# Tap work of the up stages deferred by one job on VectorE

## The chip, the core and the metric

One NeuronCore of a Trainium2 chip runs the whole program. TensorE (PE) multiplies, VectorE (DVE) and ScalarE (ACT) do the elementwise work, SyncE (SP) issues the loads of weights, GpSimd (POOL) does little here. The metric is the device time of one execution in microseconds, lower is better.

## The reference

Two transformer-like blocks on 256 positions (272 with the 16 meta positions), width 2048, all in float32. The change touches one thing in it, the feed-forward part of the first block, which is done once in each of its two layers:

```python
def causal_dwconv(x, w):
    """Causal depthwise conv over positions. x (B,L,C), w (K,C); tap K-1 = current position."""
    ...
    out = xp[:, 0:L] * w[0]
    for t in range(1, K):
        out = out + xp[:, t:t + L] * w[t]

def conv_ffn(h, w_up, dw, w_down):      # D_FF = 5632, K = 3
    u = causal_dwconv(h @ w_up, dw)
    val, gate = u[..., :D_FF], u[..., D_FF:]
    return (jax.nn.silu(gate) * val) @ w_down
```

## The kernel before

Activations lie transposed, channels on the 128 partitions and positions along the free axis, so that a product makes one tile of 128 output channels by 272 positions (258 in layer 1 of the up stages). Everything is float32, and products are made from rounded halves: a weight tile w becomes w_hi (rounded by ScalarE, line 321) and w_lo = w - w_hi (VectorE, line 327), and each tile of 128 by 128 weights takes three matmuls, x_hi with w_hi, x_lo with w_hi, x_hi with w_lo (lines 359 to 361).

The weights stream through the whole program in **parts** of at most eight 128 by 128 tiles. A part goes through four steps, each on another engine: SP loads it into `raw` (a ring of 4), ScalarE rounds it (`round_part`), VectorE subtracts (`split_part`), TensorE multiplies. `w_hi` and `w_lo` have four slots, and `AHEAD` is 3: when ScalarE and VectorE stand at part v of a stage, they prepare part v + 3, then do what follows from part v. ScalarE may round part v + 3 when TensorE is done with part v - 1. SP loads into a ring slot again when VectorE has split what lay in it.

A layer's feed-forward part is done in two halves of 22 hidden tiles each. So there are four **up stages**, called up00, up01, up10 and up11 (layer, half), each followed by a down stage. An up stage is a hardware loop of 11 iterations. One iteration has four **jobs** of two parts each, that is eight parts and 192 matmuls: u = 0 the gate of hidden tile s = 0, u = 1 its value, u = 2 and 3 the gate and the value of s = 1. Job u ends with part 2u + 1. For every job the two engines have to do this (`ffn_vector` and `ffn_scalar`):

- VectorE scales the product out of PSUM by the root, into `f_raw` (line 681), which also frees the PSUM bank;
- ScalarE makes the tap of the current position from it (line 646);
- VectorE adds the two earlier taps (line 685, two instructions);
- for a value job: ScalarE takes silu of the gate (line 650), VectorE multiplies it with the value into `f_hid` (line 695), ScalarE rounds that to `hid_hi` (line 638), VectorE subtracts to get `hid_lo` (line 672). For s = 0 these last two stand in job 2, for s = 1 they end the iteration.

The order is the order of the program on each engine, written out by `run_phase`: for each part first the preparation of part v + 3, then, if the part ends a job, the work of that job. In ScalarE's program this reads: round, round, work of job u, and so on. No step of one engine can pass an earlier one of the same engine. The down stage's first job multiplies the first 11 hidden tiles of the half, the second the other 11, and TensorE waits there for the last `hid_lo` (`hid_lo_made`). There are two PSUM banks that jobs take in turn, so the product of job u must be scaled out before job u + 2 starts.

Of the kernel before, what the change touches and what calls it, by code (L numbers as in the profile page):

```python
# [16 lines left out]
ALU = mybir.AluOpType  # L17
# [154 lines left out]
def build(nc, a, out):  # L172
# [55 lines left out]
    ps = nc.alloc_psum_tensor("ps", [P, 8, 512], F32)  # L228

    def view(buf, first, *shape):  # L230

        n = 1
        for s in shape:
            n *= s
        v = buf[:, first:first + n]
        if len(shape) == 1:
            return v
        names = "abcd"[:len(shape)]
        return v.rearrange(f"p ({' '.join(names)}) -> p {' '.join(names)}", **dict(zip(names, shape)))

    def col(name, tile=0):

        first = VOFF[name]
        if isinstance(tile, int):
            return vec[:, first + tile:first + tile + 1]
        return vec[:, first:][:, bass.ds(tile, 1)]
# [10 lines left out]
    drained = [sem(f"drained{b}") for b in range(2)]  # L257
# [69 lines left out]
        nc.vector.tensor_tensor(w_lo[:, j % SLOTS, 0:kt], raw[:, j % RING, 0:kt],  # L327
                                w_hi[:, j % SLOTS, 0:kt].bitcast(F32), ALU.subtract).then_inc(split, 1)

    def run_phase(eng, p, work, prepare, last=False):  # L330

        def body(i, on):
            for v, (u, k0, _) in enumerate(p.parts):
                if on or v + AHEAD < len(p.parts):
                    prepare(eng, p, i, v + AHEAD, p.ahead[v])
                if v == p.last[u] and work is not None:
                    work(i, u)
        n = p.n - 1 if last else p.n
        if n == 1:
            body(0, True)  # L340
        elif n > 1:
            with eng.Fori(0, n) as i:
                body(i, True)
        if last:
            body(p.n - 1, False)

    def result_ready(eng, p, i, u):

        eng.wait_ge(multiplied, i * len(p.parts) + (p.base + p.last[u] + 1 + SLOTS))
# [20 lines left out]
    def bank(name, u):  # L370
        return (results[name][0] + u) % 2
# [91 lines left out]
    def tile_of(buf, first, i, per):  # L463

        if isinstance(i, int):
            return buf[:, first + per * i]
        return buf[:, first:][:, bass.ds(i * per, 1)].rearrange("p a t -> p (a t)")
# [136 lines left out]
    f_raw, f_root = view(arena, FT0 + 8 * T, 2, T), arena[:, FT0 + 10 * T:FT0 + 11 * T]  # L604
# [22 lines left out]
    def ffn_tap(layer, f, t, is_gate, i, s):  # L627

        return col("ffn_dw", i * 2 + ((layer * FFN_K + t) * 2 * FF + is_gate * FF + f * FH + s))

    def ffn_scalar(act, layer, f):
# [8 lines left out]
        def work(i, u):  # L640
# [10 lines left out]
            if u == 3:  # L651
                high(i, 1)
        run_phase(act, p, work, round_part)
        name2 = f"down{layer}{f}"

        def squares(i, u):
            if u % 2:
# [3 lines left out]
                else:  # L661
                    square_tile(act, name2, i, u // 2, 2, 0)
        run_phase(act, ph[name2], squares if f else None, round_part)

    def ffn_vector(dve, layer, f):
        name, n0 = f"up{layer}{f}", (2 * layer + f) * FH
        p = ph[name]
        w, c = T - TAIL * layer, (FFN_K - 1) * layer

        def low(i, s):  # L670
            dve.wait_ge(hid_hi_made, i * 2 + (n0 + s + 1))
            nc.vector.tensor_tensor(tile_of(hid_lo[layer], s, i, 2)[:, 0:w - c], f_hid[:, s, c:w],  # L672
                                    tile_of(hid_hi[layer], s, i, 2)[:, 0:w - c].bitcast(F32), ALU.subtract).then_inc(hid_lo_made, 1)

        def work(i, u):
            s, is_gate = u // 2, 1 - u % 2
            if u == 2:
                low(i, 0)
            dst, raw_ = (f_gate if is_gate else f_val), f_raw[:, u % 2]
            result_ready(dve, p, i, u)  # L680
            nc.vector.tensor_tensor(raw_[:, 0:w], ps[:, bank(name, u), 0:w], f_root[:, 0:w], ALU.mult).then_inc(drained[bank(name, u)], 1)  # L681
            dve.drain()  # L682
            dve.wait_ge(hid_tap, i * 4 + (2 * n0 + u + 1))
            for back in (1, 2):
                mm = nc.vector.scalar_tensor_tensor(out=dst[:, s, back:w], in0=raw_[:, 0:w - back],  # L685
                                                    scalar=ffn_tap(layer, f, 2 - back, is_gate, i, s),
                                                    in1=dst[:, s, back:w], op0=ALU.mult, op1=ALU.add)
                if back == 1:
                    dve.drain()
            if is_gate:  # L690
                mm.then_inc(hid_tapped, 1)
            else:
                dve.drain()
                dve.wait_ge(hid_silu, i * 2 + (n0 + s + 1))
                nc.vector.tensor_tensor(f_hid[:, s, c:w], f_act[:, s, c:w], f_val[:, s, c:w], ALU.mult).then_inc(hid_made, 1)
            if u == 3:
                dve.drain()
                low(i, 1)
        run_phase(dve, p, work, split_part)
        name2 = f"down{layer}{f}"  # L700
        p2 = ph[name2]

        def low_input(i, s):


            dve.wait_ge(x0_hi_made, i * 2 + (s + 1))
            nc.vector.scalar_tensor_tensor(out=tile_of(x0_lo, s, i, 2), in0=tile_of(h, s, i, 2)[:, META:T],
                                           scalar=col("norm_w_2", i * 2 + s), in1=tile_of(x0_hi, s, i, 2).bitcast(F32),
                                           op0=ALU.mult, op1=ALU.subtract).then_inc(x0_lo_made, 1)

        def add(i, u):
            if u == 2 and layer and f:
                low_input(i, 0)
            if u % 2:
                result_ready(dve, p2, i, u)
                t = tile_of(h, u // 2, i, 2)[:, META * layer:T]
                nc.vector.tensor_tensor(t, ps[:, bank(name2, u // 2), 0:T - META * layer], t, ALU.add).then_inc(drained[bank(name2, u // 2)], 1)
            if u == 3 and layer and f:
                dve.drain()
                low_input(i, 1)  # L720
        run_phase(dve, p2, add, split_part)
# [2036 lines left out]
    with block:  # L2758
# [25 lines left out]
        @block.vector  # L2784
        def _(dve):
            start_vector(dve)
            late_vector(dve)
            dve.wait_ge(seg_made, 1)
            ab_vector(dve)
            dve.wait_ge(norm_std, 2)  # L2790
            for f in range(2):
                ffn_vector(dve, 0, f)
            meet(dve, "ffn0")
            norm_vector(dve, 2, 0, lambda k: col("norm_mix", DK + k), hi=xm_hi, lo=xm_lo)
            mid_vector(dve)
            dve.wait_ge(norm_std, 4)
            for f in range(2):
                ffn_vector(dve, 1, f)
            two_vector(dve)
            meet(dve, "out")  # L2800
            norm_vector(dve, 6, META, lambda k: col("final_norm_w_2", k), lambda k: xn[:, k, 0:S2])
            end_keep(dve, 0)
# [47 lines left out]
```

## Time and profile before

| | us |
|---|---|
| median of three runs | 3663.02 |
| lowest, highest run | 3645.42, 3664.07 |
| the profiled execution | 3644.57 |
| its span in the trace | 3642.9 |
| TensorE busy | 3506.8 (96%) |
| VectorE busy | 2364.7 (65%) |
| ScalarE busy | 1850.9 (51%) |

The profiled execution lies at the low end of the runs. The four up stages start at 409.6, 804.8, 1978.7 and 2360.8 us of the span and last 261, 260, 258 and 255 us, together 1035 us. Busy shares say what an engine does over the whole span. They don't say which engine's order sets the pace of a loop in which the engines wait for each other; for that one follows one iteration in the timeline.

### The profile page before, as it was taken

To read this page: it belongs to the slowest core of one execution; us is meant where nothing else is said; L and a number is where in the kernel's file an instruction comes from. 1 tells how busy PE (TensorE), PEld (TensorE's weight loads), DVE (VectorE), ACT (ScalarE), POOL (GpSimd) and SP (SyncE) were. 2 spreads that over 40 slices of the span, in tenths; PEclk is the share of its full clock that TensorE was granted. 3 is DMA by queue.
4 is the path that set the end of the run, shared out by engine and by line. 5 is a ranking of instruction groups with operands and counts; after the bars stand their busy time and mean duration, and the time that the engine had idled before them with its cause. 6 is when DMAs were issued, how large, how long until landed. Compare 5 with 4: busy or idle time off the path is not lost.

```text
span 3642.9 us, 76660 instructions
## 1 busy us (share of the span) xinstructions
PE 3506.8 (96%) x29352; PEld 3424.9 (94%) x29352; DVE 2364.7 (65%) x3504; ACT 1850.9 (51%) x2670; POOL 307.4 (8%) x363
## 2 busy tenths in 40 slices
PE   8989999999999899999989999999998999999998
PEld 7989999999999898888889999999997999999998
DVE  5987666657765544666656666567667657756555
ACT  4655655444444534444435555444565455475443
POOL 2761200000000000000004000000022000000000
PEclk9999999999999999999999999999998999999999
DMA  5545566566656544222225665766565556557774
GB/s 159 167 144 163 165 177 173 167 188 174 174 172 176 158 136 112 59 59 59 59 59 164 177 178 170 204 179 184 164 189 140 162 162 163 162 151 191 194 195 139
DMA packets 1103744, 561.77 MB, mean 154 GB/s; under 512 B 23044, under 2 KB 1101462, under 8 KB 1103526
## 3 DMA queue, kind: packets, MB, share of 16 engines
q1 hardware_dynamic: 1102309, 554.58, 54.1%
q8 instruction: 143, 2.34, 0.3%
q0 software_dynamic: 624, 2.13, 0.2%
q10 hardware_dynamic: 608, 2.23, 0.2%
q14 instruction: 60, 0.48, 0.0%
HBM read 556.77 MB, written 2.10 MB: 153 GB/s over the span
## 4 chain that ended last, share of the span: by engine, by line
issue 63%; PE 23%; DVE 6%; POOLq 3%; DVEq 2%; ACT 2%; DMA 0%; POOL 0%; ACTq 0%; SPq 0%
PE ps L359 5%; PE ps L360 5%; PE ps L361 5%; PE ps L443 2%; PE ps L444 2%; DVE w_lo L327 2%; PE ps L445 2%; POOLq L489 2%; DVE arena L860 1%; DVEq L682 1%; POOLq L938 1%; DVEq L854 1%; ACT w_hi L321 1%; DVE arena L685 1%; ACT arena L646 0%
## 5 line engine op out<-in xcount | busy, mean ns | idle before, releaser
L327 DVE TENSOR_TENSOR w_lo<-raw,w_hi 128x1024 fp32r<-128x1024 f32 (+1 forms) x1136 | 1351.3, 1206 | 712.2 <-ACT w_hi L321 703.2
L321 ACT ACTIVATE w_hi<-raw 128x1024 fp32r<-128x1024 f32 (+1 forms) x1136 | 1132.5, 1014 | 471.0 <-PE ps L445 249.9
L359 PE MATMUL ps<-x_hi,w_hi 128*128 128x272 f32 (+1 forms) x2816 | 804.1, 286 | 1.3 <-DVE w_lo L327 1.3
L360 PE MATMUL ps<-x_lo,w_hi 128*128 128x272 f32 (+1 forms) x2816 | 802.9, 285 | 0.0
L361 PE MATMUL ps<-x_hi,w_lo 128*128 128x272 f32 (+1 forms) x2816 | 802.8, 285 | 0.0
L443 PE MATMUL ps<-x_hi,w_hi 128*128 128x256 f32 (+2 forms) x2512 | 715.7, 285 | 45.6 <-DVE w_lo L327 31.0
L444 PE MATMUL ps<-x_lo,w_hi 128*128 128x256 f32 (+2 forms) x2512 | 706.9, 281 | 0.0
L445 PE MATMUL ps<-x_hi,w_lo 128*128 128x256 f32 (+2 forms) x2512 | 706.6, 281 | 0.0
L359 PEld LDWEIGHTS ps<-x_hi,w_hi 128*128 128x128 f32 x2816 | 533.7, 190 | 3.4 <-DVE w_lo L327 3.2
L361 PEld LDWEIGHTS ps<-x_hi,w_lo 128*128 128x128 f32 x2816 | 533.7, 190 | 0.0
L360 PEld LDWEIGHTS ps<-x_lo,w_hi 128*128 128x128 f32 x2816 | 533.7, 190 | 0.0
L443 PEld LDWEIGHTS ps<-x_hi,w_hi 128*128 128x128 f32 (+1 forms) x2512 | 475.8, 189 | 53.7 <-DVE w_lo L327 26.6
L444 PEld LDWEIGHTS ps<-x_lo,w_hi 128*128 128x128 f32 (+1 forms) x2512 | 476.4, 190 | 0.4
L445 PEld LDWEIGHTS ps<-x_hi,w_lo 128*128 128x128 f32 (+1 forms) x2512 | 476.3, 190 | 0.3
L359 PE MATMUL ps<-hid_hi,w_hi 128*128 128x272 f32 (+1 forms) x1408 | 398.7, 283 | 4.7 <-DVE hid_lo L672 4.7
L360 PE MATMUL ps<-hid_lo,w_hi 128*128 128x272 f32 (+1 forms) x1408 | 397.9, 283 | 0.0
L361 PE MATMUL ps<-hid_hi,w_lo 128*128 128x272 f32 (+1 forms) x1408 | 397.8, 283 | 0.0
L443 PE MATMUL ps<-xm_hi,w_hi 128*128 128x272 f32 (+2 forms) x944 | 290.6, 308 | 14.5 <-DVE xm_lo L584 8.6
L685 DVE SCALAR_TENSOR_TENSOR arena<-arena,vec 128x271 f32<-128x271 f32 (+1 forms) x352 | 173.9, 494 | 171.7 <-ACT arena L646 141.8
L646 ACT ACTIVATE arena<-arena,vec 128x272 f32<-128x272 f32 (+1 forms) x176 | 91.1, 517 | 379.5 <-DVE arena L681 379.5
L445 PE MATMUL ps<-xm_hi,w_lo 128*128 128x272 f32 (+2 forms) x944 | 275.7, 292 | 0.0
L444 PE MATMUL ps<-xm_lo,w_hi 128*128 128x272 f32 (+2 forms) x944 | 275.1, 291 | 0.0
(553 smaller groups left out, 5409.3 us busy)
## 6 DMA issues: line engine op xcount, KB each, us to landing
raw<-ffn_w_up SPq DMA_DIRECT2D x352, 512.0 KB, 4.5
raw<-w_in SPq DMA_DIRECT2D x232, 512.0 KB, 3.8
raw<-cd_w_in SPq DMA_DIRECT2D x100, 512.0 KB, 3.8
raw<-ffn_w_down SPq DMA_DIRECT2D x128, 384.0 KB, 3.5
raw<-ab_w_in SPq DMA_DIRECT2D x80, 512.0 KB, 3.9
raw<-ffn_w_down SPq DMA_DIRECT2D x128, 320.0 KB, 3.3
raw<-w_out SPq DMA_DIRECT2D x48, 512.0 KB, 4.3
raw<-ab_w_out SPq DMA_DIRECT2D x32, 512.0 KB, 4.0
```

The source lines that it names most:

```text
L321: nc.scalar.activation(w_hi[:, j % SLOTS, 0:kt], raw[:, j % RING, 0:kt], ACT.Copy).then_inc(rounded, 1)
L327: nc.vector.tensor_tensor(w_lo[:, j % SLOTS, 0:kt], raw[:, j % RING, 0:kt], w_hi[:, j % SLOTS, 0:kt].bitcast(F32), ALU.subtract).then_inc( ...
L359: nc.tensor.matmul(acc, w_hi[:, j % SLOTS, k, 0:w], mh, start=first, stop=False)
L360: nc.tensor.matmul(acc, w_hi[:, j % SLOTS, k, 0:w], ml, start=False, stop=False)
L361: last = nc.tensor.matmul(acc, w_lo[:, j % SLOTS, k, 0:w], mh, start=False, stop=end)
L443: nc.tensor.matmul(acc, w_hi[:, j % SLOTS, k, 0:w], mh, start=(k0 + k == 0), stop=False)
L444: nc.tensor.matmul(acc, w_hi[:, j % SLOTS, k, 0:w], ml, start=False, stop=False)
L445: last = nc.tensor.matmul(acc, w_lo[:, j % SLOTS, k, 0:w], mh, start=False, stop=(k0 + k == kt - 1))
L489: pool.drain()
L646: nc.scalar.activation((f_gate if is_gate else f_val)[:, s, 0:w], f_raw[:, u % 2, 0:w], ACT.Copy, scale=ffn_tap(layer, f, 2, is_gate, i, s ...
L682: dve.drain()
L685: mm = nc.vector.scalar_tensor_tensor(out=dst[:, s, back:w], in0=raw_[:, 0:w - back], scalar=ffn_tap(layer, f, 2 - back, is_gate, i, s), i ...
```

## The change

In the up stages VectorE's work of a job is divided. Scaling out of PSUM stays where it was, at the end of the job's second part (`work`). The wait for ScalarE's tap, the two taps, the product with silu, and for s = 0 the subtraction to `hid_lo`, go into a new function `taps` and a new hook `early`, which `run_phase` calls behind the preparation at the first part of a job: the taps of job u - 1 are then done inside job u, between the low weights of its first part's turn and those of its second part's turn. Job 3 is finished at once as before. ScalarE's, TensorE's and SP's programs are the same.

```diff
--- before.py
+++ after.py
@@ -327,12 +327,14 @@
         nc.vector.tensor_tensor(w_lo[:, j % SLOTS, 0:kt], raw[:, j % RING, 0:kt],
                                 w_hi[:, j % SLOTS, 0:kt].bitcast(F32), ALU.subtract).then_inc(split, 1)
 
-    def run_phase(eng, p, work, prepare, last=False):
+    def run_phase(eng, p, work, prepare, last=False, early=None):
 
         def body(i, on):
             for v, (u, k0, _) in enumerate(p.parts):
                 if on or v + AHEAD < len(p.parts):
                     prepare(eng, p, i, v + AHEAD, p.ahead[v])
+                if v == p.first[u] and early is not None:
+                    early(i, u)
                 if v == p.last[u] and work is not None:
                     work(i, u)
         n = p.n - 1 if last else p.n
@@ -672,14 +674,9 @@
             nc.vector.tensor_tensor(tile_of(hid_lo[layer], s, i, 2)[:, 0:w - c], f_hid[:, s, c:w],
                                     tile_of(hid_hi[layer], s, i, 2)[:, 0:w - c].bitcast(F32), ALU.subtract).then_inc(hid_lo_made, 1)
 
-        def work(i, u):
+        def taps(i, u):
             s, is_gate = u // 2, 1 - u % 2
-            if u == 2:
-                low(i, 0)
             dst, raw_ = (f_gate if is_gate else f_val), f_raw[:, u % 2]
-            result_ready(dve, p, i, u)
-            nc.vector.tensor_tensor(raw_[:, 0:w], ps[:, bank(name, u), 0:w], f_root[:, 0:w], ALU.mult).then_inc(drained[bank(name, u)], 1)
-            dve.drain()
             dve.wait_ge(hid_tap, i * 4 + (2 * n0 + u + 1))
             for back in (1, 2):
                 mm = nc.vector.scalar_tensor_tensor(out=dst[:, s, back:w], in0=raw_[:, 0:w - back],
@@ -693,10 +690,22 @@
                 dve.drain()
                 dve.wait_ge(hid_silu, i * 2 + (n0 + s + 1))
                 nc.vector.tensor_tensor(f_hid[:, s, c:w], f_act[:, s, c:w], f_val[:, s, c:w], ALU.mult).then_inc(hid_made, 1)
+
+        def early(i, u):
+            if u:
+                taps(i, u - 1)
+            if u == 3:
+                low(i, 0)
+
+        def work(i, u):
+            result_ready(dve, p, i, u)
+            nc.vector.tensor_tensor(f_raw[:, u % 2, 0:w], ps[:, bank(name, u), 0:w], f_root[:, 0:w], ALU.mult).then_inc(drained[bank(name, u)], 1)
             if u == 3:
                 dve.drain()
+                taps(i, 3)
+                dve.drain()
                 low(i, 1)
-        run_phase(dve, p, work, split_part)
+        run_phase(dve, p, work, split_part, early=early)
         name2 = f"down{layer}{f}"
         p2 = ph[name2]
```

What stands in a row on VectorE shows it. The rows name the line, the operation and its tiles; 128x1024 is the splitting of a whole part, and the register rows (ISA, REGISTER_ALU) set up addresses and the values to wait for. First, in the loop of up00, the stretch from the end of job 0's second part to the end of job 1, in the kernel before:

```order
L327 TENSOR_TENSOR w_lo<-raw,w_hi 128x1024
L349 REGISTER_ALU
L681 TENSOR_TENSOR arena<-ps,arena 128x272
L683 ISA
L685 ISA
L685 SCALAR_TENSOR_TENSOR arena<-arena,vec 128x271
L685 ISA
L685 SCALAR_TENSOR_TENSOR arena<-arena,vec 128x270
L327 TENSOR_TENSOR w_lo<-raw,w_hi 128x1024
L326 REGISTER_ALU
```

and in the changed kernel, where line 702 is the scaling and line 682 the taps:

```order
L327 TENSOR_TENSOR w_lo<-raw,w_hi 128x1024
L351 REGISTER_ALU
L702 TENSOR_TENSOR arena<-ps,arena 128x272
L327 TENSOR_TENSOR w_lo<-raw,w_hi 128x1024
L680 ISA
L682 ISA
L682 SCALAR_TENSOR_TENSOR arena<-arena,vec 128x271
L682 ISA
L682 SCALAR_TENSOR_TENSOR arena<-arena,vec 128x270
L326 REGISTER_ALU
L327 TENSOR_TENSOR w_lo<-raw,w_hi 128x1024
```

The two taps of job 0 stood directly behind its scaling, ahead of both splits of job 1; now one split stands ahead of them and one behind.

Second, the stretch from job 2's second split to the taps of job 2 and on to job 3, before:

```order
L327 TENSOR_TENSOR w_lo<-raw,w_hi 128x1024
L672 ISA
L672 TENSOR_TENSOR hid_lo_85<-arena,hid_hi_83 128x272
L349 REGISTER_ALU
L681 TENSOR_TENSOR arena<-ps,arena 128x272
L683 REGISTER_ALU
L685 ISA
L685 SCALAR_TENSOR_TENSOR arena<-arena,vec 128x271
L685 ISA
L685 SCALAR_TENSOR_TENSOR arena<-arena,vec 128x270
L327 TENSOR_TENSOR w_lo<-raw,w_hi 128x1024
L326 REGISTER_ALU
```

and now (line 674 is the subtraction to `hid_lo`):

```order
L327 TENSOR_TENSOR w_lo<-raw,w_hi 128x1024
L351 REGISTER_ALU
L702 TENSOR_TENSOR arena<-ps,arena 128x272
L327 TENSOR_TENSOR w_lo<-raw,w_hi 128x1024
L680 REGISTER_ALU
L682 ISA
L682 SCALAR_TENSOR_TENSOR arena<-arena,vec 128x271
L682 ISA
L682 SCALAR_TENSOR_TENSOR arena<-arena,vec 128x270
L674 ISA
L674 TENSOR_TENSOR hid_lo_85<-arena,hid_hi_83 128x272
L326 REGISTER_ALU
L327 TENSOR_TENSOR w_lo<-raw,w_hi 128x1024
```

The subtraction for s = 0 has moved from ahead of job 2's scaling to behind the taps of job 2, and these stand between the two splits of job 3. From job 3's scaling to the loop's end the order is the same.

## Rows read from the trace of the kernel before

**Rows 1.** The page: busy time of each engine.

```profile
PE 3506.8 (96%) x29352; PEld 3424.9 (94%) x29352; DVE 2364.7 (65%) x3504; ACT 1850.9 (51%) x2670; POOL 307.4 (8%) x363
```

**Rows 2.** Windows: up01, then up11; length, busy PE PEld DVE ACT POOL, clock, DMA.

```profile
804.80:1065.20 260.40, 260.40 (x2114) 260.40 (x2113) 181.84 (x261) 124.73 (x173) 0.00 (x0) 1.00 0.61 175
...
2360.80:2616.00 255.20, 255.20 (x2114) 255.20 (x2113) 179.44 (x261) 123.35 (x173) 0.00 (x0) 1.00 0.62 179
```

**Rows 3.** The page: costliest groups, up-stage matmuls and weight loads; last field idle before.

```profile
L359 PE MATMUL ps<-x_hi,w_hi 128*128 128x272 f32 (+1 forms) x2816 | 804.1, 286 | 1.3 <-DVE w_lo L327 1.3
...
L359 PEld LDWEIGHTS ps<-x_hi,w_hi 128*128 128x128 f32 x2816 | 533.7, 190 | 3.4 <-DVE w_lo L327 3.2
```

**Rows 4.** Timeline of PEld in up10; start, duration, idle before and its releaser.

```profile
2080.48 0.19 PEld L359 LDWEIGHTS ps<-x_hi,w_hi 128*128 128x128 f32 x1 [0.17 <-DVE w_lo L327]
...
2104.13 0.19 PEld L359 LDWEIGHTS ps<-x_hi,w_hi 128*128 128x128 f32 x1 [0.38 <-DVE w_lo L327]
```

**Rows 5.** Timeline of VectorE in up00, one iteration of the loop.

```profile
561.37 0.43 DVE L681 TENSOR_TENSOR arena<-ps,arena 128x272 f32<-128x272 f32 x1
562.63 0.50 DVE L685 SCALAR_TENSOR_TENSOR arena<-arena,vec 128x271 f32<-128x271 f32 x1 [0.82 <-ACT arena L646]
...
563.72 2.36 DVE L327 TENSOR_TENSOR w_lo<-raw,w_hi 128x1024 fp32r<-128x1024 f32 x2
565.99 0.43 DVE L681 TENSOR_TENSOR arena<-ps,arena 128x272 f32<-128x272 f32 x1
...
569.82 2.36 DVE L327 TENSOR_TENSOR w_lo<-raw,w_hi 128x1024 fp32r<-128x1024 f32 x2 [0.51 <-ACT w_hi L321]
572.09 0.43 DVE L672 TENSOR_TENSOR hid_lo<-arena,hid_hi 128x272 f32 x1
572.45 0.44 DVE L681 TENSOR_TENSOR arena<-ps,arena 128x272 f32<-128x272 f32 x1
...
577.04 0.44 DVE L681 TENSOR_TENSOR arena<-ps,arena 128x272 f32<-128x272 f32 x1
578.28 0.50 DVE L685 SCALAR_TENSOR_TENSOR arena<-arena,vec 128x271 f32<-128x271 f32 x1 [0.80 <-ACT arena L646]
...
579.60 0.44 DVE L695 TENSOR_TENSOR arena<-arena 128x272 f32<-128x272 f32 x1
...
585.27 0.43 DVE L681 TENSOR_TENSOR arena<-ps,arena 128x272 f32<-128x272 f32 x1
```

**Rows 6.** Timeline of ScalarE in up00, the same iteration.

```profile
561.94 0.52 ACT L646 ACTIVATE arena<-arena,vec 128x272 f32<-128x272 f32 x1 [1.93 <-DVE arena L681]
562.37 2.00 ACT L321 ACTIVATE w_hi<-raw 128x1024 fp32r<-128x1024 f32 x2
...
567.11 1.28 ACT L650 ACT_TABLE_LOAD   x1
568.40 0.43 ACT L650 ACTIVATE arena<-arena 128x272 f32<-128x272 f32 x1
568.74 1.99 ACT L321 ACTIVATE w_hi<-raw 128x1024 fp32r<-128x1024 f32 x2
```

**Rows 7.** Timeline of VectorE in up01.

```profile
947.05 0.44 DVE L681 TENSOR_TENSOR arena<-ps,arena 128x272 f32<-128x272 f32 x1 [0.64 <-PE ps L361]
...
953.96 0.43 DVE L681 TENSOR_TENSOR arena<-ps,arena 128x272 f32<-128x272 f32 x1
```

**Rows 8.** Timeline of PE at the end of up00.

```profile
676.94 0.40 PE L359 MATMUL ps<-hid_hi,w_hi 128*128 128x272 f32 x1 [1.79 <-DVE hid_lo L672]
```

**Rows 9.** Timeline of PE at the end of up01.

```profile
1069.74 0.39 PE L359 MATMUL ps<-hid_hi,w_hi 128*128 128x272 f32 x1 [0.26 <-DVE hid_lo L672]
```

**Rows 10.** Timeline of VectorE at the end of up00.

```profile
672.66 0.44 DVE L681 TENSOR_TENSOR arena<-ps,arena 128x272 f32<-128x272 f32 x1
```

**Rows 11.** Windows: just after that gap of PE, columns as in Rows 2.

```profile
677.60:681.10 3.50, 3.50 (x18) 3.50 (x18) 1.76 (x3) 0.91 (x3) 0.00 (x0) 0.51 0.35 105
```

## The prediction

> **What bounds the kernel now.** The page first: TensorE is busy for 96% of the span [rows 1]. Then the up stages by windows: in up01 and up11 it is busy for every microsecond [rows 2]. One iteration is 260.4 / 11 = 23.68 us there and 255.2 / 11 = 23.20 us in up11, whose tiles are 258 wide. A job is a quarter of that, 5.92 us, a part 2.96. Over all four up stages the matmuls waited 1.3 us and the weight loads 3.2 us for w_lo, 4.5 us together [rows 3]. So in these 1035 us there is next to nothing to win, and the question is the other one: how near are VectorE and ScalarE to being late?
>
> For that the timeline of one iteration in up00 is read, both engines side by side [rows 5, 6]. VectorE's scalings of jobs 0, 1, 2, 3, 0 start at 561.37, 565.99, 572.45, 577.04 and 585.27: steps of 4.62, 6.46, 4.59 and 8.23, together 23.90 us. None of these rows has an idle time that PE ended. The two engines turn in a ring, each waiting for the other, and the ring takes 23.90 us where TensorE takes 23.68. It falls back 0.22 us an iteration, living on the lead it had at the stage's start. In up10 the ring is 23.65, which is the distance of two waits of PEld for w_lo [rows 4], against PE's 23.20. The first of them is in the fifth iteration, 101.8 us into the stage: the lead was about 3 x 0.45, 1.4 us, from the second iteration on. In up01 and up11 the ring is shorter, since ScalarE loads no table there, and the scaling waits for PE (0.64 us, [rows 7]).
>
> **The change part by part.** It adds and removes no work that counts; it changes what stands in the ring. The steps, all from the rows:
> - scaling to ScalarE's tap: 561.37 to 561.94, 0.57. Tap to the next round: 562.37, 0.43 [rows 5, 6].
> - round to its split: 568.74 to 569.82, 1.08; ScalarE's second round is ready when VectorE wants it. Split to the next instruction: two take 569.82 to 572.09, so 1.14 each.
> - two taps to the next instruction: 562.63 to 563.72, 1.09. Taps to the product with silu: 578.28 to 579.60, 1.32. Subtraction to hid_lo to the next: 572.09 to 572.45, 0.36, and the product, of the same length and kind, is taken at the same.
> - silu with its table load: 565.99 to 568.40, 2.41 behind the scaling, and the round 0.34 later.
>
> Before, the taps of job 0 lie beside ScalarE's rounding: scaling, 1.26 to the taps, 1.09, then two splits, 2.28: 4.62. Now VectorE has the first split ahead of the taps, and that split needs the round, which ScalarE starts only after its tap. The taps no longer lie beside the round but behind it:
> - job 0 to 1: 0.57 + 0.43 + 1.08 + 1.14 (split) + 1.09 (taps) + 1.14 (split) = **5.45**, was 4.62.
> - job 1 to 2: 2.41 + 0.34 + 1.08 + 1.14 + 1.32 + 0.36 + 1.14 = **7.79**, was 6.46. Job 2's hid_hi is no obstacle: ScalarE makes it while VectorE does the second split.
> - job 2 to 3: 5.45 and the subtraction, 0.36 = **5.81**, was 4.59.
> - job 3 to 0: job 3 is finished at once, so **8.23** as before.
>
> The ring is 27.28 us in up00, 3.60 longer than PE's 23.68; in up10 it is taken as 0.25 less by its narrower tiles, as now (23.65 for 23.90), so 27.03, against 23.20: 3.83. In up01 and up11 ScalarE loads no table: silu can follow the tap by 0.43, as the round does in [rows 6], at 1.00 instead of 2.41, and job 3 to 0 is 947.05 to 953.96, 6.91 [rows 7]. So 5.45 + 6.38 + 5.81 + 6.91 = 24.55, which is 0.87 over 23.68; in up11 24.30, 1.10 over 23.20. There the changed ring comes out as the longer one too.
>
> What PE then waits for w_lo, at the same place in each iteration (the fourth part, whose split is the first behind the 8.23 or 6.91):
> - up00 and up10: the lead of 1.4 goes in the first iteration, which also loses about 2.4 (the first three steps, 0.83 + 1.33 + 1.22, less what was slack while PE still set the pace). 1 us and 9 x 3.60 = 33.4; 1 and 9 x 3.83 = 35.5.
> - up01 and up11: the lead is larger. The first split of job 0 starts 2.28 ahead of 953.96, at 951.68, and ends 1.22 later (2.36 - 1.14), at 952.90; PE ended the iteration just ahead of 947.05, by an estimated 0.2 us of hand-over at 946.85, and wants the fourth part 8.88 later, at 955.73. Lead 2.8 us. Ten iterations at 0.87 and 1.10, the first one less (0.4) and the second more (0.4, from a scaling that no longer catches up), make 8.7 and 11.0, less 2.8: 5.9 and 8.2.
>
> Together 83.0, less the 4.5 there was: **+78.5 us**.
>
> At a stage's end TensorE waits for the last hid_lo: 1.79 us in up00 and 0.26 in up01 [rows 8, 9], a little more in layer 1. In up00 the last scaling starts at 672.66 [rows 10], 1.7 us after the product is there, because the ring is behind. In the changed ring it is 2.28 + 5.45 + 7.79 + 5.81 = 21.33 after the fourth part's split begins; PE starts that part 1.28 after the same moment and has the job's result five parts later, at 1.28 + 14.8 + 0.2 = 16.28. Late by 5.05, 3.4 more than now. In up01: 2.28 + 5.45 + 6.38 + 5.81 = 19.92, late by 3.6 where it was not late. The down stage's first job covers 11 tiles, as now, and all of the addition shows: 2 x 3.4 + 2 x 3.7 = **+14.2 us**. After that gap of PE in up00 the clock was granted at half, 1.2 GHz, for a stretch: 18 matmuls in 3.5 us [rows 11] where 28 go in at a part's pace (24 in 2.96), some 1.3 us lost. With longer gaps I count two more such stretches, **+2.6**, bounds 0 and 5.2.
>
> VectorE's 0.82 us of idle time ahead of the taps [rows 5] goes for three jobs of four, and is worth nothing: it was beside ScalarE's rounding. PSUM banks: scaling is never over 5.1 us late, and a job lasts 5.92, so the bank wait is near but doesn't bind. Loads: a slot of raw is reloaded when its part is split, four parts ahead, over 8 us before ScalarE wants it.
>
> Sum: 78.5 + 14.2 + 2.6 = **+95 us**. Against the profiled execution's 3644.57 that is 3740; the median of the runs is 18 us above that execution, and nothing in the trace says which of the two levels the next runs take. I put the sum on the median, two of three runs being there: **3758 us**.
>
> **Rivals.**
> - *Only the stages with table loads are slowed.* The margin of 0.87 in up01 is a sum of ten steps, and if waits overlap by 0.1 each the lead lasts. Then 5.9 + 8.2 go: 3744.
> - *The clock.* A gap of 3.6 us in each iteration of up00 and up10 may halve PE's clock each time, as at the end of up00 [rows 11]. In my sum the loss is free, since after each gap PE has nothing but the ring to wait for and 3.6 us to catch up in. If it delays the scaling that the ring needs, each costs 1.3 us: 20 x 1.3 = 26, giving 3784. For it: the bank that job 3 leaves is free only 5.92 - 5.05 = 0.9 us before PE wants it. Against: a PE that runs later wants it later too, and the nearest result that the ring needs, job 1's, is there 3.3 us ahead (1.28 + 2.96 + 0.2 against 2.28 + 5.45).
> - *Not slower.* If ScalarE's round were done before VectorE asks for it, the split would cost the ring nothing, the wait of 0.82 us would be filled and the ring shorter than PE's time in every stage. Then the 4.5 us and what up00 and up10 are late by at their ends (2 x 1.7) go: 3655. It decides at the round: it would have to start ahead of the tap, and ScalarE's program puts it behind [rows 6]. A lead could also hide it, but it would have to be 36 us in up00; it is 1.4.
>
> The Trainium skill (TensorE: Matmul & The Clock Gate, "HAM oscillation — how this bites in real kernels") describes a loop whose wait in every turn puts the clock back to half each time. By it the second rival is right about the clock; by the sum it would cost nothing, by the rival 26 us. One gap in the trace agrees; none in a loop is there to look at.
>
> **How the numbers follow.** Forecast 0.70, only two stages 0.09, clock 0.10, not slower 0.11. The range: each iteration's excess is a sum of steps read to 0.02 us, and 0.3 us of error in 40 iterations is 12 us either way; the lower level of the runs takes 18 off. Low: 3758 - 18 - 14 - 12 = 3714. High: 3784 + 12 = 3796. The third rival stays out. A difference under 0.5%, some 18 us, can't be told from no change; only the third rival falls within it (faster by 0.2%), or beyond it where the next runs take the lower level, 3637. So slower 0.89, and of the rival's 0.11 same 0.08, faster 0.03.
>
> **What would show it.** Right: in up00 of the changed profile, steps of scalings near 5.45, 7.8, 5.8 and 8.2; PE idle 3.6 us once an iteration ended by w_lo, in all four stages; ScalarE's idle ahead of its tap longer by about 0.8; last hid_lo waits of 5 us. Wrong: VectorE's taps starting before the first split could be had, steps that sum to under 23.7 us, or a loop time in up01 that stays at 23.68. An error in what PE does in its gaps would show as granted clock under 1 with the iteration longer than 27.3 us.

## The result and the profile after

The changed kernel takes 3752.79 us in the median of four runs (3735.94 to 3759.50), the kernel before 3655.15 us (3645.42 to 3664.07, four runs with one more than were shown). The ratio is 1.027, interval 1.0243 to 1.0297: slower by 97.6 us in the medians, where 95 had been summed. Three single executions of kernels further below (4950, 6930 and 8878 us, where the others of the same kernel lie within 30 us) are in no ratio. The profiled execution of the changed kernel has a span of 3748.9 us, 106 more than the one before.

The page of the changed kernel first, its engine shares and the two rows that answer to [rows 3] (lines 361 and 327 are what lines 359 and 327 were; the last field is the idle time before and its releaser):

```profile
PE 3549.8 (95%) x29352; PEld 3462.5 (92%) x29352; DVE 2354.9 (63%) x3504; ACT 1850.6 (49%) x2670; POOL 306.3 (8%) x363
...
L361 PE MATMUL ps<-x_hi,w_hi 128*128 128x272 f32 (+1 forms) x2816 | 817.1, 290 | 53.9 <-DVE w_lo L327 53.8
...
L361 PEld LDWEIGHTS ps<-x_hi,w_hi 128*128 128x128 f32 x2816 | 543.6, 193 | 61.8 <-DVE w_lo L327 60.9
```

The matmuls of the up stages now wait 53.8 us for w_lo and the weight loads 60.9 us, where it was 1.3 and 3.2. The weight load and the matmul behind it wait at the same time (at 580.28 us both end their wait, after 3.43 and 3.21 us), so the two fields must not be added; the prediction did that with the 4.5 us of before, which was up to 1.3 us too much.

VectorE in one iteration of up00, the answer to [rows 5]. Start, duration, then in brackets the idle time before and what ended it; line 702 is the scaling, 682 the taps, 692 the product, 674 the subtraction to `hid_lo`:

```profile
567.26 0.43 DVE L702 TENSOR_TENSOR arena<-ps,arena 128x272 f32<-128x272 f32 x1
569.34 1.23 DVE L327 TENSOR_TENSOR w_lo<-raw,w_hi 128x1024 fp32r<-128x1024 f32 x1 [1.64 <-ACT w_hi L321]
570.48 0.49 DVE L682 SCALAR_TENSOR_TENSOR arena<-arena,vec 128x271 f32<-128x271 f32 x1
571.14 0.50 DVE L682 SCALAR_TENSOR_TENSOR arena<-arena,vec 128x270 f32<-128x270 f32 x1 [0.17 <-issue]
571.56 0.44 DVE L674 TENSOR_TENSOR hid_lo<-arena,hid_hi 128x272 f32 x1
571.91 1.22 DVE L327 TENSOR_TENSOR w_lo<-raw,w_hi 128x1024 fp32r<-128x1024 f32 x1
573.05 0.44 DVE L702 TENSOR_TENSOR arena<-ps,arena 128x272 f32<-128x272 f32 x1
...
581.28 0.44 DVE L702 TENSOR_TENSOR arena<-ps,arena 128x272 f32<-128x272 f32 x1
...
586.73 0.43 DVE L702 TENSOR_TENSOR arena<-ps,arena 128x272 f32<-128x272 f32 x1
590.55 1.22 DVE L327 TENSOR_TENSOR w_lo<-raw,w_hi 128x1024 fp32r<-128x1024 f32 x1 [3.39 <-ACT w_hi L321]
...
594.50 0.43 DVE L702 TENSOR_TENSOR arena<-ps,arena 128x272 f32<-128x272 f32 x1
```

The scalings of jobs 2, 3, 0, 1 and 2 start at 567.26, 573.05, 581.28, 586.73 and 594.50: steps of 5.79, 8.23, 5.45 and 7.77 us. Before the first split of jobs 3, 1 and 2 VectorE is idle for 1.64 or 3.39 us for ScalarE's rounding, and the taps follow that split without any wait. ScalarE's side (line 648 is the tap):

```profile
587.30 0.52 ACT L648 ACTIVATE arena<-arena,vec 128x272 f32<-128x272 f32 x1 [3.02 <-DVE arena L702]
587.84 1.28 ACT L652 ACT_TABLE_LOAD   x1
589.14 0.43 ACT L652 ACTIVATE arena<-arena 128x272 f32<-128x272 f32 x1
589.47 1.99 ACT L321 ACTIVATE w_hi<-raw 128x1024 fp32r<-128x1024 f32 x2
```

587.30 is the tap of job 1, 0.57 behind the scaling; then the table load, silu, and only at 589.47 the round that VectorE's split waits for at 590.55. The wait of VectorE for the tap, 0.82 us in [rows 5], is gone from jobs 0 to 2. In its place stands a longer wait for the round, and it lies in the ring.

TensorE in up00 at the fourth part of five iterations running, with what it had waited for:

```profile
525.80 0.60 PE L361 MATMUL ps<-x_hi,w_hi 128*128 128x272 f32 x1 [3.22 <-DVE w_lo L327]
...
553.04 0.39 PE L361 MATMUL ps<-x_hi,w_hi 128*128 128x272 f32 x1 [1.91 <-DVE w_lo L327]
...
580.28 0.59 PE L361 MATMUL ps<-x_hi,w_hi 128*128 128x272 f32 x1 [3.21 <-DVE w_lo L327]
...
607.52 0.39 PE L361 MATMUL ps<-x_hi,w_hi 128*128 128x272 f32 x1 [1.85 <-DVE w_lo L327]
...
634.76 0.60 PE L361 MATMUL ps<-x_hi,w_hi 128*128 128x272 f32 x1 [3.22 <-DVE w_lo L327]
```

Waits of about 3.2 and 1.9 us take turns. What stands behind that is shown by windows of the same places (length, busy and count of PE, PEld, DVE, ACT, POOL, granted clock, DMA):

```profile
580.00:583.40 3.40, 3.12 (x14) 3.12 (x15) 1.76 (x4) 1.54 (x3) 0.00 (x0) 0.50 0.45 129
607.40:610.80 3.40, 3.28 (x26) 3.28 (x27) 1.75 (x4) 1.71 (x3) 0.00 (x0) 1.00 0.52 147
```

Behind the 3.2 us wait at 580.28 PE runs at half clock, 0.50, 1.2 GHz: 14 matmuls in 3.4 us. Behind the 1.85 us wait at 607.52 it doesn't. The slow stretch makes PE later, so the next wait is shorter: 3.21 then 1.85. The pace stays the ring's: from 525.80 to 580.28 and from there to 634.76 it is 54.48 us each, two iterations of 27.24.

In up10 it doesn't take turns. Behind the fourth parts at 2081.87, 2108.81, 2135.75, 2162.70 and 2189.65 the clock fell every time, after waits of 3.26, 1.98 and three times 2.13 us; behind the next one, 2.12 us at 2216.59, it did not:

```profile
2108.81 0.39 PE L361 MATMUL ps<-x_hi,w_hi 128*128 128x258 f32 x1 [1.98 <-DVE w_lo L327]
...
2216.59 0.39 PE L361 MATMUL ps<-x_hi,w_hi 128*128 128x258 f32 x1 [2.12 <-DVE w_lo L327]
```

```profile
2109.20:2112.60 3.40, 3.40 (x18) 3.40 (x18) 1.77 (x3) 2.23 (x3) 0.00 (x0) 0.50 0.62 177
2216.60:2220.00 3.40, 3.40 (x28) 3.40 (x29) 1.77 (x3) 1.85 (x3) 0.00 (x0) 1.00 0.54 156
```

So the length of the wait alone doesn't say here whether the clock falls. And with a slow stretch in each of five iterations running they still take 26.94 us each, the time of the ring.

At the ends of up00 and up01, the answer to [rows 8, 9] (in up10 and up11 the same wait is 4.26 and 4.04 us, and was 2.16 and 0.48):

```profile
713.53 0.59 PE L361 MATMUL ps<-hid_hi,w_hi 128*128 128x272 f32 x1 [3.59 <-DVE hid_lo L674]
...
1114.74 0.39 PE L361 MATMUL ps<-hid_hi,w_hi 128*128 128x272 f32 x1 [3.72 <-DVE hid_lo L674]
```

### The profile page after: what moved, and what is told of

Same layout as the page of the kernel before. It is cut to its first block, busy times and chain, and to the rows that moved or that the text cites. A ratio compares the mean times of both kernels' runs of the same rounds, so it can differ in the third digit from the quotient of the medians.

```text
span 3748.9 us, 76528 instructions
## 1 busy us (share of the span) xinstructions
PE 3549.8 (95%) x29352; PEld 3462.5 (92%) x29352; DVE 2354.9 (63%) x3504; ACT 1850.6 (49%) x2670; POOL 306.3 (8%) x363
## 3 DMA queue, kind: packets, MB, share of 16 engines
q0 software_dynamic: 624, 2.13, 0.2%
## 4 chain that ended last, share of the span: by engine, by line
issue 65%; PE 14%; DVE 9%; DVEq 5%; ACT 4%; POOLq 3%; ACTq 0%; DMA 0%; POOL 0%
DVE w_lo L327 4%; ACT w_hi L321 3%; DVEq L686 2%; PE ps L361 2%; PE ps L363 2%; PE ps L362 2%; PE ps L445 2%; PE ps L446 2%; PE ps L447 2%; POOLq L491 2%; DVE arena L869 1%; POOLq L947 1%; DVE arena L682 1%; DVE arena L702 1%; DVEq L863 1%
## 5 line engine op out<-in xcount | busy, mean ns | idle before, releaser
L361 PE MATMUL ps<-x_hi,w_hi 128*128 128x272 f32 (+1 forms) x2816 | 817.1, 290 | 53.9 <-DVE w_lo L327 53.8
L362 PE MATMUL ps<-x_lo,w_hi 128*128 128x272 f32 (+1 forms) x2816 | 811.5, 288 | 0.0
L363 PE MATMUL ps<-x_hi,w_lo 128*128 128x272 f32 (+1 forms) x2816 | 811.4, 288 | 0.0
L361 PEld LDWEIGHTS ps<-x_hi,w_hi 128*128 128x128 f32 x2816 | 543.6, 193 | 61.8 <-DVE w_lo L327 60.9
L362 PEld LDWEIGHTS ps<-x_lo,w_hi 128*128 128x128 f32 x2816 | 543.3, 193 | 0.1
L363 PEld LDWEIGHTS ps<-x_hi,w_lo 128*128 128x128 f32 x2816 | 542.7, 193 | 0.0
L361 PEld LDWEIGHTS ps<-hid_hi,w_hi 128*128 128x128 f32 x1408 | 267.5, 190 | 16.6 <-issue 16.4
```

What stands on the lines that cost most here:

```text
L361: nc.tensor.matmul(acc, w_hi[:, j % SLOTS, k, 0:w], mh, start=first, stop=False)
L362: nc.tensor.matmul(acc, w_hi[:, j % SLOTS, k, 0:w], ml, start=False, stop=False)
L363: last = nc.tensor.matmul(acc, w_lo[:, j % SLOTS, k, 0:w], mh, start=False, stop=end)
```

## The experiments

Eight kernels. All timings are against the kernel before on the same chip, 19 runs of it for the first four kernels and 29 for the others. To set the up stages apart from the rest, I also took from each trace the time from the start of a stage's first matmul to the start of the last matmul of the down stage behind it, and VectorE's scaling starts, whose four steps make the ring:

| kernel | ratio (interval) | up and down stages, us: 00, 01, 10, 11 | sum less before | steps in up00, us | ring in up00, up01, up10, up11 |
|---|---|---|---|---|---|
| before | 1 | 395.0, 391.1, 382.0, 377.6 | 0 | 4.62, 6.45, 4.59, 8.23 | 23.90, 23.68, 23.66, 23.20 |
| changed | 1.027 (1.0243 to 1.0297) | 430.6, 401.3, 417.7, 390.6 | +94.5 | 5.45, 7.78, 5.79, 8.23 | 27.24, 24.50, 26.94, 24.21 |
| taps_ahead | 0.9989 (0.9970 to 1.0008) | 399.7, 391.1, 387.7, 378.2 | +11.0 | 4.62, 6.10, 5.35, 8.24 | 24.32, 23.68, 23.66, 23.20 |
| taps_behind | 1.0255 (1.0221 to 1.0288) | 431.8, 403.1, 421.6, 389.6 | +100.4 | 5.45, 7.78, 5.79, 8.23 | 27.24, 24.60, 26.94, 24.20 |
| scalar_deferred | 0.9954 (0.9934 to 0.9974) | 391.2, 391.1, 380.2, 378.3 | -4.9 | 3.71, 5.82, 5.92, 8.24 | 23.68, 23.68, 23.20, 23.04 |
| gates_only | 1.0104 (1.0074 to 1.0133) | 412.3, 391.1, 399.8, 376.9 | +34.4 | 5.45, 6.10, 5.79, 8.23 | 25.56, 23.68, 25.31, 23.20 |
| after_no_tables | 1.0111 (1.0079 to 1.0143) | 403.6, 402.4, 393.6, 391.9 | +45.8 | 5.45, 6.35, 5.79, 6.90 | 24.49, 24.50, 24.21, 24.21 |
| before_no_tables | 0.9988 (0.9968 to 1.0007) | 392.8, 391.1, 381.5, 378.3 | -2.0 | 4.93, 5.92, 5.92, 6.91 | 23.68, 23.68, 23.20, 23.04 |
| second_halves | 1.0080 (1.0056 to 1.0103) | 395.1, 402.6, 383.2, 392.7 | +27.9 | 4.62, 6.10, 4.95, 8.23 | 23.90, 24.60, 23.66, 24.21 |
| scalar_deferred_no_tables | 0.9983 (0.9963 to 1.0004) | 391.2, 391.1, 377.0, 376.9 | -9.5 | 4.92, 5.92, 5.92, 6.92 | 23.68, 23.68, 23.20, 23.20 |

Where the ring reads 23.68, 23.20 or 23.04 TensorE sets the pace, and so it does in up00 of taps_ahead with 24.32. Two things move a stage by 1 to 7 us between profiled executions, also where no edit touches it: a stretch at half clock at its start, and the pace of its matmuls at full clock (last section). A difference of that size in one stage says little by itself.

### The place of the taps: taps_ahead and taps_behind

The theory says that the loss comes from one thing: the first split, which waits for ScalarE's round, stands between ScalarE's tap and VectorE's taps. taps_ahead moves the hook by one line, ahead of the preparation:

```diff
             for v, (u, k0, _) in enumerate(p.parts):
+                if v == p.first[u] and early is not None:
+                    early(i, u)
                 if on or v + AHEAD < len(p.parts):
                     prepare(eng, p, i, v + AHEAD, p.ahead[v])
-                if v == p.first[u] and early is not None:
-                    early(i, u)
```

> The changed kernel with one thing put back: in the next job VectorE does the deferred taps ahead of the first split instead of behind it. Ring theory: the taps again lie beside ScalarE's rounding, the steps between scalings are again about 4.6, 6.1, 5.0 and 8.2 us, 23.9 in all, and the time is that of the kernel before within 5 us, ratio 1.000. Rival, that it is the division of a job's work into two places that costs (ScalarE's silu and hid_hi later), wherever the taps stand: the loss stays, ratio 1.027.

Measured 0.9989. VectorE in taps_ahead, from a scaling of job 0 to that of job 1:

```profile
589.96 0.43 DVE L702 TENSOR_TENSOR arena<-ps,arena 128x272 f32<-128x272 f32 x1
591.22 0.50 DVE L682 SCALAR_TENSOR_TENSOR arena<-arena,vec 128x271 f32<-128x271 f32 x1 [0.83 <-ACT arena L648]
591.90 0.50 DVE L682 SCALAR_TENSOR_TENSOR arena<-arena,vec 128x270 f32<-128x270 f32 x1 [0.17 <-issue]
592.31 2.35 DVE L327 TENSOR_TENSOR w_lo<-raw,w_hi 128x1024 fp32r<-128x1024 f32 x2
594.58 0.43 DVE L702 TENSOR_TENSOR arena<-ps,arena 128x272 f32<-128x272 f32 x1
```

The steps are back at 4.62 and 6.10 in the same deferred form, and the wait for the tap is back too, so that the work is divided costs nothing by itself. The stages took 11.0 us more than before, though, where 5 had been allowed. In up00 TensorE took 24.32 us an iteration, some 7 us over the stage, with no wait for w_lo in it. Up10 began with a stretch at half clock (13 matmuls from 1987.00 to 1990.00 us of the span, where the kernel before has 27 in 3 us), and its down stage had 342 matmuls in 40 us at full clock where the kernel before has 355. Neither is a wait of the ring; see the last section.

taps_behind puts the taps further on, behind both splits:

```diff
-                if v == p.first[u] and early is not None:
+                if v == p.last[u] and early is not None:
                     early(i, u)
```

> The changed kernel with the deferred taps moved further, behind both splits of the next job and just ahead of its scaling. Ring theory: a sum of the same steps (tap 0.57, round 0.43, 1.08, split, split, taps), so again about 5.45, 7.8, 5.8, 8.2 us and 27.25 in all, and the time of the changed kernel, ratio 1.027. Rival, that what costs is the second part's low weights coming later because the taps stand between the two splits: they are early again, ratio 1.00 to 1.005.

Measured 1.0255, and the steps of up00 are those of the changed kernel to 0.01 us. VectorE in taps_behind:

```profile
580.11 0.43 DVE L702 TENSOR_TENSOR arena<-ps,arena 128x272 f32<-128x272 f32 x1
582.19 2.36 DVE L327 TENSOR_TENSOR w_lo<-raw,w_hi 128x1024 fp32r<-128x1024 f32 x2 [1.65 <-ACT w_hi L321]
584.47 0.49 DVE L682 SCALAR_TENSOR_TENSOR arena<-arena,vec 128x271 f32<-128x271 f32 x1
585.14 0.50 DVE L682 SCALAR_TENSOR_TENSOR arena<-arena,vec 128x270 f32<-128x270 f32 x1 [0.17 <-issue]
585.56 0.44 DVE L702 TENSOR_TENSOR arena<-ps,arena 128x272 f32<-128x272 f32 x1
```

Both splits are now made in a row, the second part's low weights a good microsecond earlier than in the changed kernel, and it doesn't help. It is the sum of what stands in the ring that counts, not its order, as long as the first split is ahead of the taps.

### Taking the round out of the ring: scalar_deferred

If the loss is that ScalarE's round stands behind its tap, then deferring ScalarE's tap as well, to between its two rounds, must take it away and more:

```diff
-        def work(i, u):
-            s, is_gate = u // 2, 1 - u % 2
-            if u == 2:
-                high(i, 0)
+        def tap(i, u):
+            s, is_gate = u // 2, 1 - u % 2
             result_out(act, name, i, u)
...
-            if u == 3:
-                high(i, 1)
-        run_phase(act, p, work, round_part)
+        def early(i, u):
+            if u:
+                tap(i, u - 1)
+
+        def work(i, u):
+            if u == 2:
+                high(i, 0)
+            if u == 3:
+                tap(i, 3)
+                high(i, 1)
+        run_phase(act, p, work, round_part, early=early)
```

> The changed kernel, and ScalarE's tap and silu of a job deferred likewise: between its two rounds of the next job. Then the first round does not stand behind the tap. Ring theory: scaling 0.43, split 1.14, taps 1.09, split 1.14, so 3.8 for a gate job, about 5.0 for job 1 to 2, 4.2 for 2 to 3, 8.2 at the loop's end: 21.2 us, under TensorE's 23.68 and 23.20 in all four stages. The waits for low weights go, and the ends of up00 and up10 look like those of up01 and up11: 8 us under the kernel before, ratio 0.998. Rival, that VectorE's deferral costs by itself (PSUM banks or hid_lo late): ratio stays near 1.027.

VectorE in up00 of scalar_deferred (line 709 is the scaling, 689 the taps), and the page's row of the up stages' matmuls:

```profile
559.86 0.43 DVE L709 TENSOR_TENSOR arena<-ps,arena 128x272 f32<-128x272 f32 x1
560.22 1.21 DVE L327 TENSOR_TENSOR w_lo<-raw,w_hi 128x1024 fp32r<-128x1024 f32 x1
561.35 0.49 DVE L689 SCALAR_TENSOR_TENSOR arena<-arena,vec 128x271 f32<-128x271 f32 x1
562.02 0.50 DVE L689 SCALAR_TENSOR_TENSOR arena<-arena,vec 128x270 f32<-128x270 f32 x1 [0.17 <-issue]
562.43 1.22 DVE L327 TENSOR_TENSOR w_lo<-raw,w_hi 128x1024 fp32r<-128x1024 f32 x1
563.57 0.43 DVE L709 TENSOR_TENSOR arena<-ps,arena 128x272 f32<-128x272 f32 x1
...
569.38 0.44 DVE L709 TENSOR_TENSOR arena<-ps,arena 128x272 f32<-128x272 f32 x1 [0.50 <-PE ps L363]
```

```profile
L361 PE MATMUL ps<-x_hi,w_hi 128*128 128x272 f32 (+1 forms) x2816 | 802.6, 285 | 0.0
```

The step from job 0 to job 1 is 559.86 to 563.57, 3.71 where 3.8 was summed, and the next scaling waits for PE, 0.50 us. The matmuls have no idle time before them. At the end of up00 PE waits 0.27 us for hid_lo where it was 1.79 [rows 8]. The measured ratio, 0.9954, is even better than the 0.998 expected; the stages themselves gave 4.9 us, 0.13%, so most of the 17 us in the ratio does not come from there, and I don't claim it for the edit. Of the 8 us forecast, 5.6 came in up00 and up10 (3.8 and 1.8), and there up10's down stage had 342 matmuls in 40 us at full clock where the kernel before has 355. It beats the changed kernel by some 3% and is not slower than the kernel before.

### Half the dose: gates_only

```diff
         def early(i, u):
-            if u:
+            if u % 2:
                 taps(i, u - 1)
...
-            if u == 3:
+            if u % 2:
                 dve.drain()
-                taps(i, 3)
+                taps(i, u)
```

> Only the gate jobs (0 and 2) are deferred, the value jobs are finished at once. Ring theory: steps of 5.45, 6.1, 5.8, 8.2 us, 25.6 in all in up00 and 25.35 in up10, 1.9 and 2.15 over TensorE's time, so 18 and 20 us of waits for low weights and 1.7 at each end; in up01 and up11 the ring is 23.4 and 23.1, just under TensorE's time, so nothing. In all 38 us over the kernel before, ratio 1.010. Rival, a cost in proportion to the jobs deferred: two of three, 65 us, ratio 1.018.

Measured 1.0104, interval to 1.0133: the ring's 38 us, not the 65 of a cost by count. The stages lose 34.4 us: 17.3 and 17.8 in up00 and up10, and in up01 and up11 nothing, as the sum of 23.4 and 23.1 had it, under TensorE's time by 0.3 and 0.1. So a step that makes the ring longer is free up to TensorE's time and is paid in full from there on.

### The table loads: after_no_tables and before_no_tables

One line ahead of the loops of up00 and up10 brings in silu's table, so that the loop's body has no load (`warm` is a column of its own):

```diff
+        if not f:
+            nc.scalar.activation(warm[:, 0:1], eps[:, 0:1], ACT.Silu)
```

> The changed kernel with one silu of a single column on ScalarE ahead of up00 and of up10, so that the loops start with silu's table and load none in their iterations. Ring theory: the ring of up00 and up10 becomes that of up01 and up11, 24.5 and 24.2 us instead of 27.25 and 26.95, so these two stages lose what up01 and up11 lose: 48 us less than the changed kernel, ratio to before 1.0135. Rival, that the table loads are idle time of an engine that has enough of it (ScalarE is busy for half of the span) and another wait takes their place: under 10 us of change, ratio 1.025.

> The kernel before with the same single silu ahead of up00 and up10. Ring theory: the ring falls from 23.9 to 21.3 us, TensorE sets the pace in all four stages, the 4.5 us of waits for low weights and 3.4 us at the ends of up00 and up10 go: 8 us less, ratio 0.998. Rival, that the table loads cost nothing here: ratio 1.000, and the waits for w_lo still there in the profile.

In the changed kernel up00 with its down stage then takes 403.6 us and up01 402.4; the rings are 24.49 and 24.50. 45.8 us over the kernel before is left of 94.5, ratio 1.0111, in whose interval the expected 1.0135 lies. ScalarE is busy for 49% of the span, and yet 42 fewer table loads of 1.28 us are worth 94.5 - 45.8 = 48.7 us of the program's time, since they stand in the ring. (The loops had 44, two in each iteration of up00 and up10, one ahead of job 1's silu and one ahead of the first round behind the iteration's end; the two new silus have one each. The page counts 2630 ScalarE instructions for 2670, since the two silus are themselves new.) In the kernel before the same line gains 2.0 us in the stages, not the 8 forecast, and nothing that the timing can tell (0.9988): there the ring was only 0.2 and 0.45 us over TensorE's time. Against the rival, the waits for w_lo are gone (0.0 us for the matmuls, 0.2 for the weight loads) and those for the last `hid_lo` are 0.26 and 0.34 us in up00 and up10. Part of the gain is hidden by a stretch at half clock at the start of both stages, which the kernel before didn't have (in up00 15 matmuls from 410.00 to 413.00 us, where it has 27), behind the same wait of 2.0 us, and by the slower matmuls of up10's down stage, 342 in 40 us as in scalar_deferred.

### Where no table is loaded: second_halves

```diff
         def early(i, u):
-            if u:
+            if f and u:
                 taps(i, u - 1)
...
-            if u == 3:
+            if u == 3 or not f:
                 dve.drain()
-                taps(i, 3)
+                taps(i, u)
+            if u == 3:
```

> The change in up01 and up11 alone; up00 and up10 finish each job at once, except that hid_lo of the first tile stands where the change has it. Ring theory: 10 and 13 us from these two stages with their ends, ratio 1.0063, about 23 us. Rival, that only the stages with table loads can be slowed, and that in up01 and up11 the loss seen in the changed kernel came from the stage before (its lag carried over): 0 to 3 us, ratio 1.000.

Measured 1.0080, 1.0056 to 1.0103. up01 and up11 with their down stages lose 11.5 and 15.1 us, where 10 and 13 were forecast, with undisturbed stages ahead of them, so the loss in the changed kernel was their own. PE's waits in up01 and its end:

```profile
PEld ps L361 <- DVE w_lo L327: 5.9, 7, 0.9
PE ps L361 <- DVE w_lo L327: 4.4, 7, 0.7
...
PE ps L361 <- DVE hid_lo L674: 3.8, 1, 3.8
```

### Both deferred and no tables

> ScalarE's tap and silu deferred together with VectorE's taps, and no table loads in the loops. The ring is under TensorE's time without the second edit already, so ring theory gives the same as with ScalarE's deferral alone, 8 us under the kernel before, ratio 0.998. If the ring still bound somewhere, this one would be faster than that by some us.

Measured 0.9983; the stages give 9.5 us less than before. The rings were TensorE's without the second edit, and it adds nothing that can be told from the noise. Of the kernels run, scalar_deferred alone has an interval that lies wholly under 1. Since the kernel with one more edit has not, and its stages were the shorter ones, a gain over the kernel before is not shown; that the loss is gone is.

## Why the prediction was right

The time, 3752.79 us, lies between 3714 and 3796, and the difference of the medians, 97.6 us, is 2.6 us from the sum of 95. By its own steps:

- **The ring.** Forecast for up00 5.45, 7.79, 5.81, 8.23, together 27.28; measured 5.45, 7.78, 5.79, 8.23, together 27.24. up10 26.94 for 27.03, up01 24.50 for 24.55, up11 24.21 for 24.30. Every step could be read from the trace of the kernel before, though none of its iterations had them in this order.
- **The stages.** With their ends and the clock the sum gave about 36, 11, 35 and 13 us for the four; measured 35.6, 10.2, 35.7 and 13.0. The waits begin where the leads were said to end: in up00 in the second iteration, in up01 in the fifth.
- **What the waits were.** The total held better than its terms. Of the 83.0 us of waits for w_lo the weight loads show 60.9. In the loops of up00 and up10 the clock was at half in five and seven stretches behind such waits; in them PE was slow instead of idle, some 19 us in all (an estimate, 12 times the 1.55 us of the next point). The ring takes its time either way, and so the stages came out as summed.
- **The stage ends.** up01's last wait became 3.72 us, forecast 0.26 + 3.6. In up00 it is 3.59 and not 5.2, since PE itself was late from a stretch at half clock: from the fourth part to the last matmul ahead of the wait it took 20.40 us, in up01 18.85, that is 1.55 more. The ring's time of arrival is as summed. Over the four ends the waits grew by 10.9 us, where 14.2 had been put.
- **The clock.** Two further stretches at half clock behind the ends, of up01 and up11, as counted. In the loops the clock fell too, in every second iteration of up00 and in five iterations running of up10. The Trainium skill (TensorE: Matmul & The Clock Gate, "HAM oscillation — how this bites in real kernels") tells of a loop in which it falls in every turn; this trace agrees for those five turns of up10, and not for up00, where it fell behind the waits of 3.2 us and not behind those of 1.9 between them. The rival's 26 us did not come: two iterations of up00 take 54.48 us with one slow stretch in them, which is twice the ring, and those of up10 26.94 with one in each. The loss fell into time in which PE would have waited.
- **The rivals.** That only the stages with table loads are slowed fell by second_halves. That the round is ready in time fell by the 1.64 and 3.39 us waits; made true by scalar_deferred, it does what that rival said, the waits for w_lo gone.
- **What the sum didn't have.** Of the 106 us between the two profiled executions 94.5 are in the feed-forward stages. The other 11.5 are 15.7 in the second block, by the last section's effect, less some 4 elsewhere. The 18 us between the runs of one kernel the prediction left without a cause, and they still have none that is shown. It put 95 on 3663, and the runs of the kernel before now have a median of 3655, 8 us lower; the difference came out 2.6 larger, and so 3758 is 5 us above the time. Which level the next runs would take was a guess, and it was said to be one.
- **What would show it.** The waits of 3.6 us once an iteration in all four stages, named there, did not come: they are 3.2 and 1.9 in up00, 1.0 to 3.3 in up10, and 0.5 to 0.75 in up01 and up11, where the prediction's own excess of 0.87 and 1.10 us an iteration leaves no room for 3.6. Nor did the last waits of 5 us; they are 3.6 to 4.3.

One point was argued and not tried: that the PSUM banks, free 0.9 us ahead, hold. No wait for them shows up in the profile after, but none was provoked either.

## What to carry to other kernels

Where two in-order engines hand work to and fro, write down one turn of the ring, step by step, and compare it with the bottleneck's time for the same turn; busy shares (63% and 49% here) say nothing about it. Moving dependent work later frees its waiting engine only if the work that now goes first doesn't itself depend on the other engine's next step; if it does, two things that lay side by side are put in a row. Here deferring the partner's side by the same step took the loss away.

## What was not expected of the hardware

The same matmuls at the same granted clock take one of two pitches, by the execution and the stretch. Windows of 40 us in the second block, with 256 columns, no waits and clock 1.00, before and after:

```profile
3360.00:3400.00 40.00, 40.00 (x356) 40.00 (x355) 22.14 (x26) 18.16 (x23) 2.21 (x3) 1.00 0.73 196
```

```profile
3460.00:3500.00 40.00, 40.00 (x342) 40.00 (x341) 21.64 (x25) 16.33 (x23) 1.47 (x2) 1.00 0.68 186
```

356 matmuls in 40 us, and 342: 112.4 and 117.0 ns each (those that reach over an edge of the window are counted too). The starts in the traces have a median distance of 113 or 118 ns for hundreds of matmuls at a time, and change over at a few places, other ones in other executions; over the block's last 600 us or so the changed kernel's profiled execution was at 118 throughout, the one of the kernel before at 113 in most of it, which is 15.7 us between the two over the block. The kernels second_halves and scalar_deferred_no_tables, whose code in this block is the same, were at 118 there throughout, scalar_deferred at 113 for about the last two thirds. In the up stages there is the like: PE's own iteration of 192 matmuls takes 23.68 us or, in up00 of taps_ahead, 24.32, that is 123.3 or 126.7 ns each; and in up11 23.20 or 23.04, 120.8 or 120.0 ns each. The windows of up00, of the kernel before and of taps_ahead:

```profile
500.00:540.00 40.00, 40.00 (x327) 40.00 (x326) 26.85 (x42) 22.81 (x30) 0.00 (x0) 1.00 0.59 172
```

```profile
500.00:540.00 40.00, 40.00 (x318) 40.00 (x318) 26.50 (x39) 23.45 (x31) 0.00 (x0) 1.00 0.59 168
```

This is of the size of the 18 us between the runs of one kernel, whose granted clock is the same at either end (3645.34 and 3671.17 us, both with a mean of 0.987). That the pitch makes them is not shown, since no kernel was profiled both at a short and at a long run, and what sets the pitch stays open. It also says that differences of under 0.5% between single profiled executions have to be read stage by stage, and with the pitch taken off.
